# Two gate tiles of the pooling branch computed six chunks earlier, inside the paged stage

## The reference

```
h = rms_norm(x)
q, k, v, u, ga, gp = split(h @ w_in)           # each 1024 wide
o = attention(q, k, v)                         # prompt: causal; sample: 8 pages of 128 cached keys per sequence
for g, w in enumerate((2, 4, 8, 16)):          # on u, 256 channels each
    d = (cumsum window of w) / count - u
    pool_o[g] = (d @ w_pool[g]) * pool_scale[g]
merged = sigmoid(ga) * (o @ w_attn_branch) + sigmoid(gp) * (pool_o @ w_pool_branch)
x1 = x + merged @ w_out
y  = x1 + conv_ffn(rms_norm(x1))
```

## Time and profile before

| | |
|---|---|
| median of three runs | 2094.36 us |
| profiled execution | 2096.5 us |
| span of its trace | 2094.7 us |
| granted clock of PE, mean | 0.985 |
| PE busy | 2041.9 us (97%) |
| DVE, ACT, POOL busy | 1125.2, 615.3, 487.0 us |
| moved by DMA | 187.74 MB, 90 GB/s over the span |

### The profile page before, as it was taken

One profiled execution on the slowest core, in us unless ns is written; L12 is line 12 of the kernel. 1 busy time (PEld: TensorE's weight loads), 2 busy tenths in 40 slices (PEclk: granted clock), 3 DMA queues, 4 the chain that ended last, 5 costly groups with the idle time before them and its releaser, 6 DMA issues.

```text
span 2094.7 us, 33677 instructions
## 1 busy us (share of the span) xinstructions
PE 2041.9 (97%) x13113; PEld 1858.2 (89%) x13113; DVE 1125.2 (54%) x1499; ACT 615.3 (29%) x1216; POOL 487.0 (23%) x339
## 2 busy tenths in 40 slices
PE   9999999999988878999999999999999999999999
PEld 8888888888867766999999988999999999999997
DVE  6766666665632433366553434555555455555556
ACT  5444544445411111224112322221221122122120
POOL 4333333332100000342332111211221122022110
PEclk9999999999988989999999999999999999999999
DMA  4222212124499996312224410110121111112112
GB/s 151 57 62 57 62 41 57 33 62 132 121 271 281 273 285 211 92 41 61 87 80 135 150 37 25 57 42 31 51 62 31 41 51 41 31 51 62 31 41 97
DMA packets 189120, 187.74 MB, mean 90 GB/s; under 512 B 11680, under 2 KB 154540, under 8 KB 188852
## 3 DMA queue, kind: packets, MB, share of 16 engines
q1 hardware_dynamic: 155068, 142.42, 23.1%
q10 hardware_dynamic: 33920, 43.43, 7.0%
HBM read 161.68 MB, written 24.35 MB: 89 GB/s over the span
## 4 chain that ended last, share of the span: by engine, by line
PE 93%; DMA 4%; DVE 1%; SPq 1%; ACT 0%; ACTq 0%; issue 0%; POOL 0%; POOLq 0%; DVEq 0%
PE PS L1498 39%; PE PS L2265 13%; PE PS L1032 6%; PE PS L2020 5%; PE PS L288 4%; PE PS L290 4%; PE PS L289 4%; PE PS L344 3%; DMA v_pg<-in_cache_v_dram 3%; PE PS L368 3%; PE PS L357 2%; PE PS L1102 1%; PE PS L1136 1%; PE PS L1519 1%; PE PS L1531 1%; PE PS L323 1%
## 5 line engine op out<-in xcount | busy, mean ns | idle before, releaser
L1485 POOL TENSOR_TENSOR fw_lo<-fw_raw,fw_hi 128x1024 fp32r<-128x1024 f32 x86 | 216.1, 2512 | 941.4 <-ACT fw_hi L1481 941.4
L1498 PE MATMUL PS<-m_hi,fw_hi 128*128 128x384 f32 (+1 forms) x1032 | 228.1, 329 | 0.0
L1498 PE MATMUL PS<-m_lo,fw_hi 128*128 128x384 f32 (+1 forms) x1032 | 227.4, 328 | 0.0
L1498 PE MATMUL PS<-m_hi,fw_lo 128*128 128x384 f32 (+1 forms) x1032 | 227.4, 328 | 0.0
L2393 DVE TENSOR_TENSOR x<-x,PS 128x512 f32<-128x512 f32 x198 | 136.2, 688 | 142.8 <-PE PS L2265 142.5
L1498 PEld LDWEIGHTS PS<-m_hi,fw_lo 128*128 128x128 f32 x1032 | 176.3, 188 | 0.0
L1498 PEld LDWEIGHTS PS<-m_lo,fw_hi 128*128 128x128 f32 x1032 | 176.2, 188 | 0.0
L1498 PEld LDWEIGHTS PS<-m_hi,fw_hi 128*128 128x128 f32 x1032 | 175.9, 188 | 0.2
L288 PE MATMUL PS<-w_hi,act_hi 128*128 128x384 f32 (+1 forms) x456 | 164.7, 361 | 0.0
L290 PE MATMUL PS<-w_hi,act_lo 128*128 128x384 f32 (+1 forms) x456 | 153.6, 337 | 0.0
L289 PE MATMUL PS<-w_lo,act_hi 128*128 128x384 f32 (+1 forms) x456 | 153.1, 336 | 0.0
(11 more groups left out here) (318 smaller groups left out, 4220.5 us busy)
## 6 DMA issues: line engine op xcount, KB each, us to landing
k_ring<-in_cache_k_dram SPq DMA_DIRECT2D x256, 128.0 KB, 4.4
v_pg<-in_cache_v_dram ACTq DMA_DIRECT2D x51, 512.0 KB, 11.2
fw_raw<-in_w_up_dram SPq DMA_DIRECT2D x44, 512.0 KB, 4.1
wd_raw<-in_w_down_dram SPq DMA_DIRECT2D x22, 512.0 KB, 4.2
w_raw<-in_w_in_dram SPq DMA_DIRECT2D x21, 512.0 KB, 5.2
out_dram<-raw SPq DMA_DIRECT2D x16, 512.0 KB, 3.7
fw_raw<-in_w_in_dram SPq DMA_DIRECT2D x12, 512.0 KB, 4.0
fw_raw<-in_w_in_dram ACTq DMA_DIRECT2D x12, 512.0 KB, 8.0
```

The lines of the kernel that those rows point to most:

```text
L1485: e.tensor_tensor(fw_lo[slot][:, 0:kts, :], fw_raw[:, 0:kts, :], fw_hi[slot][:, 0:kts, :].bitcast(F32), ALU.subtract).then_inc(fw_tail, 1)
L1498: ins = e.matmul(PS[:, 3 * slot + c, 0:cw], w[slot][:, kt, :], x[:, kt, c0:c0 + cw], start=first and kt == 0, stop=last and kt == KT - 1)
```

## The change

- `N_FP`, the gate tiles of the pooling branch that are fill tiles, goes from 6 to 8: `N_FILL` is 16, and the stage N_GP is gone. The eight tiles of the map now have the numbers right behind those of u.
- The paged stage holds six more chunks. `P_EACH` is (7, 5, 5, 5, 5, 4, 4, 3). The chunks of a batch are divided by `split_chunks`: two first, half of the others (rounded down) between, the others rest. `P_PROBS` is 0, so the list behind the probabilities is empty. By batch: between 2, 1, 1, 1, 1, 1, 1, 0 and rest 3, 2, 2, 2, 2, 1, 1, 1.
- PE goes from the last tile of u to the map. SP loads the two weight blocks of the map before it stores the rows of u; the wait of DVE for these stores stands at map tile 5, the first whose low part lies over `u_rows` in SBUF.
- The two more gate tiles are spilled and read back like the others; ACT applies the sigmoid to eight tiles in the u loop.

```diff
-        N_FP = 6
+        N_FP = KT
         N_FILL = N_FP + KT
-        N_U, N_GP, N_PL, N_PB, N_AB, N_UP = N_FILL, N_FILL + KT, 3 * KT, 4 * KT, 5 * KT, 6 * KT
+        N_U, N_PL, N_PB, N_AB, N_UP = N_FILL, N_FILL + KT, 4 * KT, 5 * KT, 6 * KT
-        P_EACH = (6, 5, 4, 4, 4, 4, 3, 2)
+        P_EACH = (7, 5, 5, 5, 5, 4, 4, 3)
+        P_PROBS = 0
+        def split_chunks(fill):
+            mid = 2 + P_PROBS + (len(fill) - 2 - P_PROBS) // 2
+            return fill[0:2], fill[2:2 + P_PROBS], fill[2 + P_PROBS:mid], fill[mid:]
...
# PE and ACT, by batch
-                for f in fill[2:3]:
+                for f in between:
                     f()
                 for j in range(KEY_GROUP, NPG + 1):
                     pe_value_page(e, b, j)
-                for f in fill[3:]:
+                for f in rest:
                     f()
...
# pe_phase3
-            pe_fm_tile(e, N_GP, 0, act_hi, act_lo)
             u_rows_transpose(KT - 1)
-            pe_fm_tile(e, N_GP + 1, 1, act_hi, act_lo)
             e.wait_ge(ur_copied, KT)
...
# act_phase3
-                if m < N_FP:
-                    e.activation(sig_p[:, m, :], sig_p[:, m, :], ACT.Sigmoid)
+                e.activation(sig_p[:, m, :], sig_p[:, m, :], ACT.Sigmoid)
-            fm_head(e, N_GP + 1, 1)
-            gate(N_GP, KT - 2, 0)
             act_u_rows(e, KT - 1)
...
             d_parts(range(D_FIRST))
-            fm_head(e, N_PL, 0)
-            gate(N_GP + 1, KT - 1, 1)
             d_parts(range(D_FIRST, D_AHEAD))
...
# dve_phase3
-            e.wait_ge(ur_st, UR_STORES * 16)
             for m in range(KT):
+                if m == PO_OVER_U_ROWS:
+                    e.wait_ge(ur_st, UR_STORES * 16)
...
# sp_phase3
-            for i in range(2):
-                fm_load(e, N_GP + i, w_in_cols(COL_GP + (N_FP + i) * P))
+            for k in range(POOL_LOADS):
+                e.wait_ge(fw_tail, N_PL + k)
+                e.dma_start(fw_raw[...], w_pool[0, 2 * k:2 * k + 2]...).then_inc(fw_ld, 16)
             e.wait_ge(ur_copied, KT)
             e.dma_start(pool_prompt[0, 0], u_rows[NSAMP:NSAMP + BUF, :]).then_inc(ur_st, 16)
```

More of the change, by code:

```diff
@@ L1149, in pe_phase2 @@
             for b in range(NB):
-                fill = [lambda p=p: pe_chunk(e, p, {}) for p in chunks_of(b)]
+                first, after_probs, between, rest = split_chunks([lambda p=p: pe_chunk(e, p, {}) for p in chunks_of(b)])
                 pe_new_scores(e, b)
@@ L1153, in pe_phase2 @@
                 if b == 0:
-                    fill[0]()
+                    first[0]()
                 pe_page_scores(e, b, 1)
                 if b:
-                    fill[0]()
-                fill[1]()
+                    first[0]()
+                first[1]()
                 pe_probs(e, b)
+                for f in after_probs:
+                    f()
                 for j in range(KEY_GROUP):
                     pe_value_page(e, b, j)
-                for f in fill[2:3]:
+                for f in between:
                     f()
@@ L1194, in act_phase2 @@
             for b in range(NB):
-                fill = chunks_of(b)
+                first, after_probs, between, rest = split_chunks(chunks_of(b))
                 if b == 0:
-                    act_chunk(e, fill[0])
+                    act_chunk(e, first[0])
                 act_sample_exp(e, b)
                 if b:
-                    act_chunk(e, fill[0])
-                act_chunk(e, fill[1])
+                    act_chunk(e, first[0])
+                act_chunk(e, first[1])
+                for p in after_probs:
+                    act_chunk(e, p)
                 act_load_values(e, b, 0, KEY_GROUP)
-                for p in fill[2:3]:
+                for p in between:
                     act_chunk(e, p)
@@ L1206, in act_phase2 @@
                 act_take_values(e, b)
-                for p in fill[3:]:
+                for p in rest:
                     act_chunk(e, p)
@@ L1383, in build_step @@
         sp_rows = r("sp_rows", [NB * BUF, D])
+        PO_OVER_U_ROWS = (r.at - R2U) // fit(TOK)
         u_rows = r("u_rows", [NSAMP + BUF, D])
@@ L1652, in act_phase3 @@
                     e.wait_ge(gp_ld, 16)
-                if m < N_FP:
-                    e.activation(sig_p[:, m, :], sig_p[:, m, :], ACT.Sigmoid)
-            def gate(n, m, slot):
-                fm_done(e, n)
-                for ps, lo, hi in fm_parts(slot):
-                    ins = e.activation(cols(sig_p[:, m, :], lo, hi), ps, ACT.Sigmoid)
-                ins.then_inc(fm_free, 1)
-            fm_head(e, N_GP + 1, 1)
-            gate(N_GP, KT - 2, 0)
+                e.activation(sig_p[:, m, :], sig_p[:, m, :], ACT.Sigmoid)
             act_u_rows(e, KT - 1)
@@ L1869, in pool_phase3 @@
                 e.tensor_copy(u_col[m % 2][:, NSAMP:NSAMP + BUF], x[:, SEQ:SEQ + BUF]).then_inc(ucol_ready, 1)
-            fm_tail(e, N_GP + 1, 1)
             pool_rstd_o(e, step, 0)
-            for k in range(POOL_LOADS):
-                fm_tail(e, N_PL + k, k)
+            fm_tail(e, N_PL + 1, 1)
             fm_tail(e, N_PB, 0)
@@ L1935, in sp_phase3 @@
                 fm_load(e, N_U + m, w_in_cols(COL_U + m * P))
-            for i in range(2):
-                fm_load(e, N_GP + i, w_in_cols(COL_GP + (N_FP + i) * P))
+            for k in range(POOL_LOADS):
+                e.wait_ge(fw_tail, N_PL + k)
+                e.dma_start(fw_raw[:, :, :].rearrange("p (k a) b -> p k (a b)", a=2),
+                            w_pool[0, 2 * k:2 * k + 2].rearrange("g (kt p) n -> p (g kt) n", p=P)).then_inc(fw_ld, 16)
             e.wait_ge(ur_copied, KT)
@@ L1941, in sp_phase3 @@
                 e.dma_start(pool_sample[0, b, BUF - NS:BUF, :], u_rows[b * NS:(b + 1) * NS, :]).then_inc(ur_st, 16)
-            for k in range(POOL_LOADS):
-                e.wait_ge(fw_tail, N_PL + k)
-                e.dma_start(fw_raw[:, :, :].rearrange("p (k a) b -> p k (a b)", a=2),
-                            w_pool[0, 2 * k:2 * k + 2].rearrange("g (kt p) n -> p (g kt) n", p=P)).then_inc(fw_ld, 16)
             for m in range(2):
```

## The result

Four runs of the changed kernel took 2107.69 us in the median (2104.35 to 2108.23), four of the kernel before on the same chip 2093.78 us (2090.0 to 2094.56). The ratio is 1.0067, with a 95% interval of 1.0049 to 1.0084: slower by 13.9 us, 10 to 18 by the interval. Predicted were 2104.7 us and a range of 2096 to 2113. Between the two profiled executions (2096.5 and 2107.68 us) the difference is 11.2 us; the prediction's sum was 10.3. That the whole came out close doesn't mean that each part did, so the parts are compared first.

A forecast was written before the change was run, and what follows sets the result against it. PE's matmuls were taken to carry nearly all the time, the wait for value pages being the other visible share. Terms 14.0 + 3.0 + 0 - 6.7 = +10.3 us took the median from 2094.4 to 2104.7 us, range 2096 to 2113.

The forecast's parts named there:

- The four chunks of rest, +14.0: Paged stage, batches 2, 3, 4 and 6: each added chunk behind the value pages costs 3.5 us, +14.0 in all.
- Test (a): Batches 2 to 4: starts of scores 3 to 4 us further apart, scores to last value page still 26 to 28.
- More bytes, +3.0: Paged stage: two more weight loads and five more spilled chunks, 1.95 MB, cost +3.0 us, bounds -1 and +7.
- test (b): Batches 1 and 6: the time from scores to the last value page grows by some 3 us.
- Test (c): End of the paged stage: the scores of batch 7 start near 832 us, not 815.5.
- End of the stage, 0: First tile of u: batch 7's added chunk is absorbed by idle time and regained clock; 0 us, bounds -1 and +2.
- test d: First tile of u: PE has no idle time there any more.
- The map, -6.7: Between u and map: without gate tiles the map starts 8.2 us sooner, less 1.45 us of clock loss; -6.7 us.
- test (e): Before the map: a gap of 15 to 18 us, ended by DVE's low part, with slow matmuls behind it.
- The byte pace: Rival, chance 0.10: bytes pace the paged stage at 273 GB/s, 1.95 MB cost 7.1 us; +3.9 in all, 2098.3 us.
- The rival that waits give back what rest takes: Chance 0.07: first parts of batches shrink as second parts grow, only batch 6's chunk is paid; -3.2 us, 2091.2 us.
- ACT's queue: Rival, chance 0.08: ACT waits longer for spills, value requests come late in two or three batches; +18 us, 2112 us.

The follow-up runs named there:

- the map's part alone: Kernel before, with the last two gate tiles left out and the map right behind u, paged stage unchanged; 2086.22 against 2094.70 us, ratio 0.9963.
- the run with four sets: The changed kernel, with the scores of batch 0's new keys computed four times instead of once; 2105.04 against 2094.02 us, ratio 1.0062.

## Why the prediction was right, and where it was not

**The four chunks of rest, +14.0.** Right in mechanism and nearly in size. The second parts of the four batches grew by 15.6 us, 3.9 a chunk instead of 3.5, inside the bounds of 12 and 16. Test (a) asked for scores 3 to 4 us further apart behind batches 2, 3 and 4, with first parts of 26 to 28 us. The first parts are 26.3 to 27.1 us; the distances grew by 1.1, 4.0 and 1.6 us against the earlier trace rows, because there batches 2 and 4 had been 27.7 and 30.3 us long. Against the trace of the map's part alone, the same stage run once more, they grew by 3.3, 2.5 and 4.0. So the test holds roughly against one trace of the old stage, and for batch 3 alone against the other. The chunks moved between the pages turned the term round, so it is the place that sets it.

**More bytes, +3.0.** The amount was plausible, the argument wrong. The failed step is "in batch 4 the weight load is issued 3.9 us ahead of the value requests ... +3.5 us": a load added there cost 1.0 us or less in the trace, and in the change batches 4 and 6, with the load ahead, took 27.1 and 28.4 us, not 3 more than the rest; test (b) failed for batch 6. At 1 us for a MB the 1.95 MB are worth 2 us, at the medians of the added loads some 2 us more. What batch 4 of the kernel before spends its 30.3 us on is not settled. The versions with added bytes have 29.0 to 33.3 us there, the map's part alone 28.3, and none was aimed at it.

**What the prediction didn't have.** The first part of batch 1 took 10.9 us more. It came with the pause and left with it (27.9 us with one chunk fewer in batch 0, 26.6 with the longer stream). In the six kernels with seven chunks in batch 0 and the pause in batch 1 the part took 32.3 to 36.5 us, 34.2 on the mean, in the six with six chunks in batch 0 25.6 to 28.1, mean 27.0; so of the 10.9 us some 7 are typical, and the change's trace is the longest of its kind. Of the 10.9 us, 3.3 are the pause, 1.0 the three slow matmuls of scores behind it, 2.4 those of the chunks (10.27 for 7.88), and the rest lies mostly in the wait for the last value page (12.20 us on the chain for 7.93). ACT asks for the first of the values 22.1 us after the scores began, in the run with four sets 15.4 us after (ACT in order of time, the change first):

```profile
623.93 3.55 ACTq L1304 DMA_DIRECT2D v_pg<-in_cache_v_dram  x4
```

```profile
621.35 3.55 ACTq L1305 DMA_DIRECT2D v_pg<-in_cache_v_dram  x4
```

So of the 9.85 us between these two runs' batches 6.74 lie before the request, and 3.11 between the request and the last page; the DMA share was 1.07 and 1.06 in these stretches, and why the page took longer isn't shown. Against it stands that batch 0 ended 3.4 us sooner, though it holds one chunk more (between the pages, which the prediction put at nothing; why it ends sooner, no run was aimed at), and that the first parts of batches 2 to 6 were 3.0 us shorter (1.6 against the other trace of the old stage). In net, 4.5 us stand in the place of the predicted 3.0. That they lie so near is luck: a loss of 10.9 us that the prediction didn't know met gains that it didn't know either. Test (c) was met by it, with 835.7 for the forecast 832.

The price of the pause to the whole kernel is open. In the traces, the run with four sets of new scores starts the scores of batch 7 6.8 us sooner than the change (828.89 and 835.66), though it does 1.4 us more; in medians it is only 2.7 us better, with intervals that overlap.

**End of the stage, 0.** Right: 1.2 us came back, of the 1.45 that the clock had cost, and PE no longer waits for the pooling rows (test d).

**The map, -6.7.** Right. The gap is 16.25 us, as test (e) had it, and closed by 8.5 us, 8.2 predicted, since the delay of DVE beside POOL was gone whole and not by two thirds. The prediction read three sums of 2.16 us each where one took 3.52; the term is the same. The map's matmuls took 26.49 us where they had taken 24.93, +1.56 for the clock after the pause, 1.45 predicted. Together -6.9, and the map alone measured 7.8 us faster (5 to 11).

**The sum.** 20.2 - 1.2 - 8.5 + 1.6 = 12.1 us to the end of the map (12.0 by the chain), 11.2 to the end of the kernel.

**The rivals.** The byte pace is refuted: the same bytes with the chunks in another place took 16 us less, and added stores cost about a quarter of its price per MB. The Trainium skill, "DMA: Bandwidth & Descriptors", section "Where 436 GB/s comes from", has about 358 GB/s as one core's part of the memory. No run here was held at it: the stage moved 261 and 273 GB/s in the two kernels, and a window of two microseconds in the run with four sets of new scores 417 (below), so over such a stretch it was no ceiling.

```profile
602.00:604.00 2.00, 2.00 (x13) 2.00 (x12) 0.00 (x0) 1.44 (x2) 0.42 (x1) 1.00 1.04 417
```

The rival that waits give back what rest takes fell with chunks in rest: batches 3 and 5 got no shorter, and batch 4 by 3.2 us alone. But it has a small part of truth in both directions, 1.6 to 3.0 us of relief in the change and 6.0 of 18.1 us taken back when the rest was moved between the pages. ACT's queue cost nothing that was found: in batch 1 it waits 9.5 us for a spill, until 609.59, and its exponentials then still wait for DVE until 611.71.

## What to carry to other kernels

Work that is moved under a wait has to be placed ahead of what ends the wait: the same chunks cost 2.5 to 4.9 us each behind the last page and about 1.5 between the pages. A price that is read from one odd batch (30.3 us in batch 4) is not the price of the thing that happens to stand there; look for the same thing elsewhere, or add it alone. Two traces of the same stage differed by 2 us in one batch, so a term of that size needs more than one trace. And a stage that is started sooner gives its gain back if the queue of the engine that feeds it is only turned round (4.7 us won, 4.1 lost again); with the late work woven in, 2 to 3 us stayed.

## What the runs showed of the hardware

- PE paused at places that lie multiples of 128 matmul records apart in its stream, for 1.8 to 4.5 us where the 128 ahead were small (2 to 3.6 us of work) and the DMA share was 0.8 to 1.1, for 0.3 to 2.0 us at later places of the same kind (share 1.0 to 1.1), and not at all with a share of 0.28. Its queue of instructions had 98, 99, 100 and 101 packets for 12969, 13113, 13209 and 13369 matmul records. Adding 96 small ones, 1.4 us of work, moved the pause out of batch 1.
- 5.1 MB of stores added to a stage with a DMA share of 0.96 cost 4.0 to 4.9 us, about a quarter of what 273 GB/s would make of them.
- One of three alike sums of about 128 x 1220 on DVE took 3.52 us beside POOL's subtraction, the others 1.42 and 1.48; without the subtraction the three took 4.38.
- After a pause of 16 us, and after one of 1.8, the same 1.5 us were lost to the clock; after the one of 3.3 us in the change's batch 1 it was 3.4 us (three matmuls of scores and 48 of chunks).
